# Reordering the first pass of the projections: two pairs scaled at the banks, the norms one product later, sums of weights on GpSimd

## The reference, cut to what matters

```
def rmsnorm(x, g):
    xf = x.astype(F32)
    r = lax.rsqrt(jnp.mean(xf * xf, axis=-1, keepdims=True) + EPS)
    return (xf * r * g.astype(F32)).astype(x.dtype)
...
xn = rmsnorm(x, p['g_mix'][l])
proj = xn @ p['w_in'][l]
```

## Time and profile before

| | us |
|---|---|
| median of 3 runs | 2885.44 (2883.5 to 2887.72) |
| the profiled execution | 2884.78, of which 2883.0 is its span |
| PE busy in the span | 2745.6 (95%) |
| steps 0 to 7 and half of step 8 (0 to 250 us) | PE busy 197.60 of 250.00, mean granted clock 0.91 |
| the rest of the second pass (250 to 366 us) | PE busy 115.02 of 116.00, mean granted clock 1.00 |
| start of the first block product | 18.30 |

### The profile page before, as it was taken

One profiled execution on the slowest core, in us unless ns is written; L12 is line 12 of the kernel. 1 busy time (PEld: TensorE's weight loads), 2 busy tenths in 40 slices (PEclk: granted clock), 3 DMA queues, 4 the chain that ended last, 5 costly groups with the idle time before them and its releaser, 6 DMA issues. The chain is left out here.

```text
span 2883.0 us, 46671 instructions
## 1 busy us (share of the span) xinstructions
PE 2745.6 (95%) x16778; PEld 2639.3 (92%) x16778; DVE 1881.8 (65%) x2933; ACT 1381.3 (48%) x2627; POOL 438.4 (15%) x657
## 2 busy tenths in 40 slices
PE   5889999999999999999989999999999999999997
PEld 4778889999998989999989999999999998999997
DVE  6765556767767667777887777856544456555554
ACT  3344334554555455555654444674433367333442
POOL 3220011222122212222210000020000003001112
PEclk9999999999999999999999999999999999999998
DMA  4543366555755448778675666667655566755665
GB/s 163 162 150 105 115 192 192 186 163 187 226 179 163 146 160 258 263 261 266 217 275 202 224 218 216 232 221 258 201 184 178 187 196 205 244 189 191 201 192 122
DMA packets 386388, 568.60 MB, mean 197 GB/s; under 512 B 54322, under 2 KB 212466, under 8 KB 386162
## 3 DMA queue, kind: packets, MB, share of 16 engines
q1 hardware_dynamic: 384050, 565.49, 60.4%
q10 hardware_dynamic: 2112, 0.13, 0.0%
HBM read 414.90 MB, written 151.62 MB: 197 GB/s over the span
## 5 line engine op out<-in xcount | busy, mean ns | idle before, releaser
L2601 PE MATMUL f_ps<-f_xt,f_wh 128*128 128x348 f32 (+1 forms) x3696 | 670.5, 324 | 18.9 <-DVE both_high L3030 12.8
L2601 PEld LDWEIGHTS f_ps<-f_xt,f_wh 128*128 128x128 f32 x3696 | 604.9, 190 | 24.7 <-DVE both_high L3030 17.8
L2944 DVE TENSOR_TENSOR f_wl<-both_high,f_wh 128x512 fp32r<-128x512 f32 (+1 forms) x494 | 357.5, 737 | 205.1 <-ACT f_wh L2694 201.6
L2694 ACT ACTIVATE f_wh<-both_high 128x512 fp32r<-128x512 f32 (+1 forms) x494 | 298.7, 621 | 341.3 <-PE f_ps L2606 265.0
L2601 PE MATMUL f_ps<-f_gbuf,f_wh 128*128 128x348 f32 (+1 forms) x2112 | 383.7, 322 | 15.5 <-ACT f_ps L2807 6.3
L2606 PE MATMUL f_ps<-f_xt,f_wl 128*128 128x348 f32 (+1 forms) x1848 | 371.9, 323 | 0.5 <-DMA f_wl<-up_parts 0.5
L2601 PEld LDWEIGHTS f_ps<-f_gbuf,f_wh 128*128 128x128 f32 x2112 | 342.7, 188 | 21.0 <-ACT both_low L2812 10.0
L2606 PEld LDWEIGHTS f_ps<-f_xt,f_wl 128*128 128x128 f32 x1848 | 309.9, 189 | 0.7 <-DMA f_wl<-up_parts 0.7
L1054 PE MATMUL pp<-gxh,gwh 128*128 128x416 f32 x792 | 291.3, 368 | 1.3 <-DVE gxl L1003 1.3
L1054 PE MATMUL pp<-gxh,gwl 128*128 128x416 f32 x792 | 279.7, 353 | 0.0
L1054 PE MATMUL pp<-gxl,gwh 128*128 128x416 f32 x792 | 278.4, 351 | 0.0
(11 more groups left out here) (365 smaller groups left out, 4657.7 us busy)
## 6 DMA issues: line engine op xcount, KB each, us to landing
both_high<-in_w_up SPq DMA_DIRECT2D x220, 256.0 KB, 4.1
f_wh<-up_parts SPq DMA_DIRECT2D x176, 256.0 KB, 2.7
f_wl<-up_parts SPq DMA_DIRECT2D x176, 256.0 KB, 3.1
both_low<-in_w_gate SPq DMA_DIRECT2D x80, 512.0 KB, 4.5
up_parts<-f_wh SPq DMA_DIRECT2D x88, 256.0 KB, 3.0
up_parts<-f_wl SPq DMA_DIRECT2D x88, 256.0 KB, 3.4
both_high<-in_w_br SPq DMA_DIRECT2D x40, 512.0 KB, 4.9
both_high<-in_w_out SPq DMA_DIRECT2D x40, 512.0 KB, 4.4
```

The source lines that it names most:

```text
L2601: pe.matmul(out, cut(wh, k), x(k), start=(start and k == 0 and x is xhi), stop=False, skip_group_check=not start or not stop)
L2694: act.activation(ring_slot(wh, e, w), src, ACT.Copy).then_inc(ev("w_hi"), 1)
L2944: dve.tensor_tensor(ring_slot(wl, e, w), src, ring_slot(wh, e, w).bitcast(F32), ALU.subtract).then_inc(ev("w_lo"), 1)
```

## The change

- **Start.** SP loads the first chunk, g_mix and b11 before the second chunk and the constants. The gains of pair 0 are done by DVE (`first_gains`), and PE no longer does `sums(0)` and `rows(0)` before its first product.
- **Pairs 0 and 1** are split and multiplied with their gains only. Their results are multiplied by the root when they leave the banks (`scaled_quarter`, placed by `QUARTERS`), by a scale per partition. Their `normed` still takes place, later, for the copy in memory.
- **Norms.** `NORMS` puts the sample rows after pair 3. Squares, reduces, sums, rows and norms are placed later: for pairs from 4 on, the squares at (p-2, 5) and (p-2, 6) where they were at (p-2, 4) and (p-2, 5); the reduces at (p-2, 6) and (p-1, 0); the sums at (p-1, 1) where they were at (p-1, 0). The splits of a pair move from two to three products into the step before.
- **Reduce** is three additions on DVE of 512, 256 and 128 elements, each waiting for the one before, for one tensor_reduce of 1024.
- **Sums of weights.** t3 of the first pass and t3, t2, t4 of the second move from DVE to POOL; the splits of the second half of the weights come in another order.
- **Stores and loads** of SP are reordered to match; the roots have a place of their own for each pair, so a wait on the buffer of roots falls away.

```
-W_OPS = [(0, t) for t in ("b11", "b21", "b12", "b22", "t3", "t1", "t2", "t4")] + [(1, x[1]) for x in STRASSEN]
+W_OPS = [(0, t) for t in ("b11", "b21", "b12", "b22", "t3", "t2", "t1", "t4")] + [(1, t) for t in ("b11", "t3", "b21", "t1", "t2", "b22", "t4")]
-NORMS = [0, 1, "s", *range(2, PAIRS_A)]
+NORMS = [0, 1, 2, 3, "s", *range(4, PAIRS_A)]
+LATER = range(4, PAIRS_A)
+ACT_SQUARES = after([((1, 0), (0, 4)), ((1, 1), (0, 5)), ((2, 0), (1, 2)), ((2, 1), (1, 3)), ((3, 0), (2, 0)), ((3, 1), (2, 0)), (("s", 0), (2, 3))]
+                    + [((p, i), (p - 2, 5 + i)) for p in LATER for i in range(2)])
+REDUCES = after([((1, 0), (0, 5)), ((1, 1), (0, 5)), ((2, 0), (1, 3)), ((2, 1), (1, 3)), ((3, 0), (2, 0)), ((3, 1), (2, 1)), (("s", 0), (2, 4))]
+                + [((p, i), (p - 2 + i, 6 * (1 - i))) for p in LATER for i in range(2)])
+SUMS = after([(0, (0, 4)), (1, (1, 1)), (2, (1, 4)), (3, (2, 2)), (4, (2, 5))] + [(p + 1, (p - 1, 1)) for p in LATER])
+ROWS_AT = after([(0, (0, 5)), (1, (1, 2)), (2, (1, 5)), (3, (2, 3)), (4, (2, 6))] + [(p + 1, (p - 1, 2)) for p in LATER])
+VARIANCES = SUMS
+NORMED = after([(0, (0, 6)), (1, (1, 3)), (2, (1, 5)), (3, (2, 3)), (4, (2, 6))] + [(p + 1, (p - 1, 2)) for p in LATER])
 X_SPLITS = after([((1, "a11"), (0, 6)), ((1, "a21"), (0, 6)), ((1, "a12"), (0, 7)), ((1, "a22"), (0, 7))]
+                 + [((2, t), w) for t, w in zip(("a11", "s3", "s2", "a12", "s1", "a22", "s4"), ((1, 6), (1, 6), (1, 7), (1, 7), (2, 0), (2, 0), (2, 1)))]
+                 + [((e, x[0]), (step_of(e) - 1 + (j + 3) // 7, (j + 3) % 7)) for e in range(3, ENTRIES) for j, x in enumerate(STRASSEN)])
+W_SPLITS = after([((0, "t3"), (1, 0)), ((0, "t2"), (1, 2)), ((0, "t1"), (2, 0)), ((0, "t4"), (2, 1))]
+                 + [((1, t), w) for t, w in zip(("b11", "t3", "b21", "t1", "t2", "b22", "t4"), ((7, 1), (7, 2), (7, 4), (7, 5), (7, 6), (8, 0), (8, 1)))])
+QUARTERS = after([((0, "c11", 0), (0, 6)), ((0, "c21", 1), (0, 6)), ((0, "c12", 2), (0, 7)), ((0, "c22", 3), (1, 0)),
+                  ((1, "c11", 0), (1, 3)), ((1, "c21", 1), (1, 3)), ((1, "c12", 4), (1, 6)), ((1, "c22", 3), (1, 7))])
...
+        def scaled_quarter(s, t, m):
+            done(s, {"c11": 2, "c21": 3, "c12": 6, "c22": 7}[t])
+            act.wait_ge(ev("rtok_ready"), NORM_AT[s] + 1)
+            wait(act, "out_" + t, 16 * s)
+            x = 2 * NORM_AT[s] + int(t[1]) - 1
+            act.activation(out[t], ps[m][:, 0:HALF], ACT.Identity, scale=rtok[:, x:x + 1]).then_inc(ev(t), 1)
...
         square(0, 0)
+        x_high(0, "a11")
+        w_high(0, "b11")
         square(0, 1)
-        w_high(0, "b11")
-        x_high(0, "a11")
...
-            dve.tensor_reduce(ssum[:, i, 0:w], xsq[:, :, 0:w].rearrange("p k t -> p t k"), AX.X, ALU.add).then_inc(ev("ssum_ready"), 1)
+            for x, k in enumerate((4, 2)):
+                wait(dve, "squares_added", 2 * q + x)
+                dve.tensor_tensor(xsq[:, 0:k, 0:w], xsq[:, 0:k, 0:w], xsq[:, k:2 * k, 0:w], ALU.add).then_inc(ev("squares_added"), 1)
+            wait(dve, "squares_added", 2 * q + 2)
+            dve.tensor_tensor(ssum[:, i, 0:w], xsq[:, 0, 0:w], xsq[:, 1, 0:w], ALU.add).then_inc(ev("ssum_ready"), 1)
...
+        first_gains(0)
+        x_low(0, "a11")
         reduce(0, 0)
-        reduce(0, 1)
-        variance(0)
         w_low(0, "b11")
-        normed(0)
-        x_low(0, "a11")
+        first_gains(1)
         x_low(0, "a21")
         w_low(0, "b21")
         x_low(0, "a12")
         x_low(0, "a22")
+        reduce(0, 1)
...
     @block.gpsimd
...
         for h, g in enumerate(NORMS):
             n = 1 if g == "s" else 2
             if h == 0:
+                t3_sum_of(0)
+            else:
+                for i in range(n):
+                    gains(g, i)
+            if h == 1:
                 t1_sum_of(0)
+            roots(h, n)
...
+        t3_sum_of(1)
         t1_sum_of(1)
+        pool.wait_ge(ev("w_lo"), W_AT[1, "t3"] + 1)
+        weights_in(pool, "b11", 1)
+        pool.tensor_tensor(t_sum, t_sum, raw["b11"], ALU.subtract).then_inc(ev("t2_ready"), 1)
+        pool.wait_ge(ev("w_lo"), W_AT[1, "t2"] + 1)
+        weights_in(pool, "b21", 1)
+        pool.tensor_tensor(t_sum, raw["b21"], t_sum, ALU.add).then_inc(ev("t4_ready"), 1)
```

More of the change, by code:

```diff
@@ L135 @@
 SQ_END = [max(i for i, u in enumerate(SQUARES) if u[0] == g) + 1 for g in NORMS]
[L136 to L140, removed]
@@ L291, in ahead @@
                              ).then_inc(next_ev(f"gw_in{u}"), 16)
-        x_load(0)
+        chunk_load(0, 0)
+        sp.dma_start(gmix[:], a["g_mix"]).then_inc(ev("g_in"), 16)
+        weights(0, "b11")
+        chunk_load(0, 1)
         sp.dma_start(ident, a["consts"][:, CAT["ident"][0]:CAT["ident"][1]]).then_inc(ev("cst_in"), 16)
         sp.dma_start(ones, a["consts"][:, CAT["ones"][0]:CAT["ones"][1]]).then_inc(ev("cst_in"), 16)
-        sp.dma_start(gmix[:], a["g_mix"]).then_inc(ev("cst_in"), 16)
-        for t in ("b11", "b21", "b12", "b22"):
+        for t in ("b21", "b12", "b22"):
             weights(0, t)
@@ L306, in _ @@
                 x_load(s + 1)
[L307 to L311, removed]
+            if s + 1 < PAIRS_A:
+                normed_out(s + 1)
+            if s == 2:
+                sp.wait_ge(ev("blank"), 1)
+                for i in range(8):
+                    sp.dma_start(prs[CHUNKS][SAMP:P, 225 * i:225 * i + 225], blank[SAMP:P, :]).then_inc(ev("samp_out"), 16)
+            if s == 3:
                 sp.wait_ge(ev("xn_ready"), SQ_AT["s", 0] + 1)
                 sp.dma_start(xns[:, :, SEQ:SEQ + SAMP], xs[:]).then_inc(ev("xs_out"), 16)
[L314 to L338, removed]
+                sample_out(0)
+                for t in ("b12", "b22", "b11", "b21"):
+                    weights(1, t)
+            if s == AHEAD_A:
+                sample_out(1)
+                ahead()
+            for t in ("c11", "c22", "c21", "c12"):
+                rows_out(s, t)
         sp.wait_ge(ev("xs_out"), 16)
@@ L534, in normed @@
             wait(dve, "rb_done", h + 1)
+            if g in range(CLASSIC):
+                wait(dve, "x_lo", X_END[g])
             for i in range(1 if g == "s" else 2):
@@ L566, in x_low @@
                 x_sums(e, t)
-        def t3_sum(h):
-            weights_in(dve, "b12", h)
-            weights_in(dve, "b22", h)
-            wait(dve, "w_lo", W_AT[h - 1, "t4"] + 1 if h else 0)
-            dve.tensor_tensor(t_sum, raw["b12"], raw["b22"], ALU.subtract).then_inc(ev("t3_ready"), 1)
         def w_low(h, t):
```

102 lines of the change are left out of this document (56 added, 46 removed).

## The result

| | before | after |
|---|---|---|
| median, us | 2885.44 | 2899.44 (2898.44 to 2903.41, 5 runs) |
| the profiled execution | 2884.78 | 2903.41, the slowest of its five |
| ratio to before | | 1.005, 95% interval 1.0035 to 1.0064 |
| first block product starts | 18.30 | 11.32 |
| first matmul of the next stage (the mixer) starts | 376.23 | 391.56 |

The change costs 14.0 us; 2896 was forecast, +10.8.

A forecast was written before the change was run, and what follows sets the result against it. PE, busy 95% of the span, bounds the kernel. Pauses 51.4 against 36.2 (+15.2), start -9.3, `sums` and `rows` of pair 0 +0.9, clock +4.0: together +10.8, so 2896 us; 8-in-10 range 2872 to 2908.

The forecast's parts named there:

- the walk: Step-by-step estimate through the four engine queues: 2896 us, own range 2889 to 2904, chance 50%.
- The lock between DVE and POOL: A two-SBUF-input DVE instruction starting while POOL works stands still until POOL ends: 2.39 us for one of 0.69.
- The test I named: The walk is wrong if additions keep to 1.4 us beside POOL, or step 2's pause is under 8 us.
- The three rivals: Long sums don't block DVE (2874 us, 15%); nor do gains (2865, 7%); only short additions slip through (2887, 20%).
- the first rival: POOL's long weight sums do not hold DVE up, its queued instruction going first: 2874 us, chance 15%.
- Step 2: Pause before the sums of pair 3: 16.1 us of queued work against 4.9 of products, so 11.2 us.
- Steps 4, 5 and 6: Pauses at the sums, chunk 0's reduce standing behind the split of a12: 3.6 us each.
- Step 8: Second pass: product (8, 4) waits for seeds queued on ACT behind the weight sums and splits: 4.5 us.
- Start: First product at 8.95 instead of 18.30 us, b11 landing near 7.2: a gain of 9.3 us.
- Steps 0 and 1: First-pass pauses: a21 0.4, a12 of pair 0 5.0, `rows(0)` 0.3, pair 1 5.6, pair 2 5.7 us.
- The second pass: After the step 8 wait nothing changes; line 606 is 4.5 us behind product 3 and wanted at 4.9.
- The clock: Lower clock after pauses over 2 us, 2.0 us each, ten against eight before: +4.0 us (2.8 to 5.2).

The follow-up runs named there:

- e2: Changed kernel with pair 3's squares and reduces placed earlier and the split of t1 a product later: 2893.19 us, ratio to before 1.0032.
- e8: Changed kernel with the transfers behind b11 held back until the first chunk of x has landed: 2896.5 us, a single run.
- e9: e6 with the transfers behind b11 held back in the same way as in e8: 2864.86 us, ratio to before 0.9927.
- e4: Changed kernel with squares, reduces, sums, rows, norms and splits from pair 5 on placed as before the change: 2893.28 us, ratio to before 1.0038.
- e6: Changed kernel with the edits of e2, e3 and e4, and tensor_reduce for chunks due together with POOL's gains: 2865.29 us, ratio to before 0.994.
- e3: Changed kernel with weight sums back on DVE, except first-half t1 (later on POOL) and second-half t3 (on POOL): 2890.91 us, ratio to before 1.0018.

## Why the prediction was right about the sign and short in size

The direction and the range held: 2899.4 lies in 2872 to 2908 and in the walk's own 2889 to 2904. By its own steps:

- **The lock between DVE and POOL** was right where it was priced from the earlier trace rows: a12, pair 1, and the gains beside the additions. The test I named, additions that keep to 1.4 us beside POOL, did not come out so. The three rivals without the lock, or with it for long instructions only, are refuted as rules. But the turn at a12, which I took for certain, is not: once, in e2, DVE's split went first, as the first rival had it, and that was worth some 3 us by the `sums` of pair 2.
- **Step 2** was 10.64 for 11.2, and e2 shows that order, not POOL, makes it. Steps 4, 5 and 6 were 3.50, 3.98 and 3.45 for 3.6 each. Step 8 was 4.45 for 4.5 and the samples 2.82 for 3.0. The two in step 4 and (6, 6) were 3.14 and 1.53 for 2.8 and 2.1. The 6.1 us that I counted to pair 1 of the kernel before belong to the sample rows, whose `sums` stood behind (1, 0) there: moved behind pair 3 they cost 2.82. The total of 36.2 is not touched by it.
- **Start: -7.0 for -9.3.** The step that failed is "0.66 MB less lie ahead of b11, so it lands near 7.2". Bytes ahead are not all: b11 landed at 9.55, 7.9 us after its issue, where the same block took 5.8 before. e8 and e9 give some 0.85 us of it to transfers issued behind. The rest of the delay, some 1.5 us, is open.
- **Steps 0 and 1: 12.9 for 17.0** (a12 3.44 for 5.0, pair 1 4.86 for 5.6, `rows` of pair 1 2.31 for none and, with that delay in it, pair 2 2.32 for 5.7; the 0.4 at a21 and the 0.3 at `rows(0)` are absent). I had DVE held by POOL, but not POOL's small diagonals held by DVE and PE by them. In all the pauses of the first pass were 46.4 for 51.4.
- **The second pass: +2.4 for 0.** "Afterwards nothing changes" was wrong, though not by line 606, whose slack of 0.4 us I weighed in a rival: it is a store that ACT waits for, once, at 309 us. e4 puts it down to the later places.
- **The clock: +9.4 for +4.0.** This is the term that was mis-sized most. Summed over the stage, four matmuls of 450 columns that follow each other slower than every 0.82 us, with the pauses taken out, lose 20.3 us before and 29.7 after. The size per pause was right: about 2.1 us on average in both kernels, beside my 2.0. The number was not: 12 pauses cost 1.5 us or more where 8 did before and 10 were forecast, since the stall of step 4, the one at `rows` of pair 1 and the one in the second pass are long enough too. Length alone does not decide: behind the stall of 2.42 us before and behind the 1.53 at (6, 6) only 0.1 us was lost. The start's own restart lost 2.8 for 1.4.

The account closes: start -7.0, pauses of the first pass +10.2, of the second +2.4, the clock +9.4, together +15.0 of the 15.3 us by which the mixer starts later. `sums` and `rows` of pair 0 between the products, +0.9 in the forecast, delay them by 0.6 (the products behind them start 0.36 and 0.24 after them) and are in neither sum, so such an account is good to about 1 us. For e6 against before: start -7.8, pauses of the first pass -12.3 (23.9 for 36.2), the clock -2.3 (18.0 for 20.3), together -22.4 of -23.0.

So the gain at the start was real, and three other parts each cost as much or more than its 7.0 us: the sums on GpSimd 14.3 us (an estimate of 11 where the turn at a12 falls as in e2, 14.3 less 3.4), the place of pair 3's squares 7.1, the later norms and splits 7.3 to 7.9. Which of the 7.3 is the squares' and which the splits' places was not separated.

## What to carry to other kernels

A shorter stretch on one engine is worth nothing beside the order of the queues: before an operation is moved to an idle engine, list which instructions of the busy one it locks out or is locked out by, and who waits behind them. Where a pause goes, look for the next chain of the same queue, which will take part of it back (pair 2 here took back 5.7 of the 9.2 us that e3 won ahead of it). And count every pause twice, once for itself and once for the clock after it, some 2 us for most of them in this stage, down to those of 1.7 us. Last, where two engines that lock each other out ask at the same moment, one profile shows one outcome of several: compare kernels from a point that they reach alike.

## What the runs showed of the hardware that was not expected

- DVE and POOL hold each other up in turns, so the smallest instruction can pay most: 4.02 us for an addition of 0.29, and 3.77 for two diagonals of 0.76. Which goes first can differ between kernels of the same order: the sum is recorded from 0.11 us before the end of DVE's low part in after and in e2 alike, and DVE's next split came behind it in after and ahead of it in e2.
- A transfer seems to be slowed by those issued behind it: 900 KB took 7.1 to 8.0 us from issue to landing with a chunk of x issued 0.5 us later, and 6.6 and 7.0 with that and all behind it held back.
- The part of the program behind the stage, the same in all kernels, took 2506.8 to 2513.9 us in the eleven profiles, so a change of 2 to 3 us in the stage is lost in the total. The stage's own end shows it only if no turn between DVE and POOL fell otherwise, which was worth some 3 us here.
